# Latent attention: a unit's roots spread ahead of the weighing and scaled ahead of the next means, and a first preparation with each unit's chain in one step

## What is computed

```python
q = split_heads(rms_norm(c_q, mla_cq_norm) @ mla_w_uq, MLA_HEADS)
kv = split_heads(rms_norm(c_kv, mla_ckv_norm) @ mla_w_ukv, MLA_HEADS)
k_nope, v = jnp.split(kv, [MLA_NOPE_DIM], axis=-1)
k = jnp.concatenate([k_nope, k_rope_h], axis=-1)
q = rms_norm(q, mla_q_norm)
k = rms_norm(k, mla_k_norm)
q = jnp.concatenate([q[..., :MLA_NOPE_DIM], rope(q[..., MLA_NOPE_DIM:], cos, sin)], axis=-1)
k = jnp.concatenate([k[..., :MLA_NOPE_DIM], rope(k[..., MLA_NOPE_DIM:], cos, sin)], axis=-1)
o_mla = merge_heads(block_causal_attention(q, k, v)) @ w_branch_mla
g_fox, g_mla = jnp.split(jax.nn.sigmoid(gate_logit + b_gate), N_BRANCH, axis=-1)
```

## Time and profile before

| | us |
|---|---|
| median of 3 runs (2532.12 to 2543.33) | 2540.17 |
| the profiled execution | 2539.42 |
| its span, first to last instruction | 2537.6 |
| PE busy in the span | 2395.9 (94%) |
| DVE busy | 1423.5 (56%) |
| ACT busy | 958.0 (38%) |
| POOL busy | 508.5 (20%) |
| mean granted TensorE clock, as a share of full speed | 0.967 |

### The profile page before, as it was taken

How to read it: one execution, slowest core, us unless ns; L and a number is a source line. 1 busy time by engine, 2 the same in 40 slices (tenths; PEclk the granted TensorE clock), 3 DMA queues, 4 the chain that set the end, 5 groups by cost and what they waited for, 6 DMA issues and landing times. The chain is left out here.

```text
span 2537.6 us, 36864 instructions
## 1 busy us (share of the span) xinstructions
PE 2395.9 (94%) x14060; PEld 2124.4 (84%) x14060; DVE 1423.5 (56%) x2057; ACT 958.0 (38%) x1621; POOL 508.5 (20%) x632
## 2 busy tenths in 40 slices
PE   6899999999978999989899999989989999999999
PEld 6899999999968888878677777778877888887887
DVE  7655655655554574572455555544276666556553
ACT  5333333333334454442343333353343333334332
POOL 0032300000022442440233333332410332000000
PEclk8999999999988899989999999989999999999999
DMA  5356633375421000001111111023613656427553
GB/s 187 119 190 216 208 127 105 145 273 184 144 83 52 26 1 25 26 1 36 37 50 37 37 40 36 26 96 132 237 54 132 226 192 213 139 69 276 207 200 109
DMA packets 132698, 297.99 MB, mean 117 GB/s; under 512 B 10096, under 2 KB 57072, under 8 KB 129216
## 3 DMA queue, kind: packets, MB, share of 16 engines
q1 hardware_dynamic: 132544, 295.88, 33.6%
HBM read 206.99 MB, written 88.72 MB: 117 GB/s over the span
## 5 line engine op out<-in xcount | busy, mean ns | idle before, releaser
L1070 DVE TENSOR_TENSOR f_w_lo<-f_rw,f_w_hi 128x1024 fp32r<-128x1024 f32 x154 | 195.2, 1267 | 222.2 <-ACT f_w_hi L590 222.2
L833 PE MATMUL f_ps<-u_hi,f_w_hi 128*128 128x260 f32 (+1 forms) x1056 | 283.7, 323 | 25.9 <-DVE f_w_lo L1070 13.1
L833 PE MATMUL f_ps<-u_lo,f_w_hi 128*128 128x260 f32 (+1 forms) x1056 | 283.0, 323 | 0.0
L833 PE MATMUL f_ps<-u_hi,f_w_lo 128*128 128x260 f32 (+1 forms) x1056 | 282.7, 322 | 0.0
L590 ACT CAST f_w_hi<-f_rw 128x1024 fp32r<-128x1024 f32 x154 | 161.2, 1047 | 164.4 <-PE f_ps L833 157.2
L833 PE MATMUL f_ps<-f_far_hi,f_w_hi 128*128 128x260 f32 (+1 forms) x792 | 211.9, 322 | 8.7 <-DVE f_ev L1086 8.7
L833 PEld LDWEIGHTS f_ps<-u_hi,f_w_hi 128*128 128x128 f32 x1056 | 178.3, 192 | 42.2 <-DVE f_w_lo L1070 14.6
L833 PE MATMUL f_ps<-f_far_lo,f_w_hi 128*128 128x260 f32 (+1 forms) x792 | 210.9, 321 | 0.0
L833 PE MATMUL f_ps<-f_far_hi,f_w_lo 128*128 128x260 f32 (+1 forms) x792 | 210.7, 321 | 0.0
L833 PEld LDWEIGHTS f_ps<-u_lo,f_w_hi 128*128 128x128 f32 x1056 | 177.8, 192 | 14.3
L833 PEld LDWEIGHTS f_ps<-u_hi,f_w_lo 128*128 128x128 f32 x1056 | 177.7, 192 | 14.1
(11 more groups left out here) (392 smaller groups left out, 5954.0 us busy)
## 6 DMA issues: line engine op xcount, KB each, us to landing
f_rw<-in_gu SPq DMA_DIRECT2D x88, 512.0 KB, 4.4
f_rw<-kept_dsum SPq DMA_DIRECT2D x32, 704.0 KB, 4.7
f_rw<-kept_hid SPq DMA_DIRECT2D x33, 520.0 KB, 5.6
f_rw<-in_down SPq DMA_DIRECT2D x24, 704.0 KB, 4.3
f_rw<-kept_hid SPq DMA_DIRECT2D x33, 512.0 KB, 5.4
h_in<-in_wd SPq DMA_DIRECT2D x11, 1024.0 KB, 6.7
kept_dsum<-h_in SPq DMA_DIRECT2D x44, 256.0 KB, 3.0
h_out<-in_wd SPq DMA_DIRECT2D x11, 1024.0 KB, 7.2
```

Source lines behind the costliest of these rows:

```text
L833: last = nc.tensor.matmul(out[:, b, 0:N], w[:, c], u[:, b * N:(b + 1) * N], start=(j < 3 and k == 0 and i == 0), stop=(k == 3 and i == 2), ...
L1070: nc.vector.tensor_tensor(slot(w_lo, st), src, slot(w_hi, st).bitcast(F32), ALU.subtract).then_inc(wlo_done, 1)
```

## The change

In the heads, the spread of unit w-1 moves on PE from behind the sums of unit w to ahead of the weighing. On ACT the copy of the roots of unit w-1 moves ahead of the root of unit w. On DVE the means of unit w move from ahead of the rounding of the scores to behind the scaling of unit w-1, and the rotation (now `turn`) stands behind the means. In the first preparation each unit's projection, sums, spread and scaling all stand in one step, the rounding of unit w-1 stands ahead of the squares of unit w on ACT, and the tables of groups and of logit copies are new. Nothing is added or left out; only the order changes.

```diff
@@ tables of the first preparation
-        FIRST = {(w, x): 2 if 2 <= w < 6 else 1 - x if w >= 6 else 0 for w in range(14) for x in range(2)}
-        FIRST.update({(0, 0): 1, (0, 1): 5, (1, 0): 2})
+        FIRST = {(w, x): 0 for w in range(-1, 14) for x in range(2)}
+        FIRST.update({(-1, 0): 1, (-1, 1): 4, (0, 0): 1, (0, 1): 2, (5, 0): 1, (5, 1): 1})
+        FIRST.update({(w, x): 1 + 2 * x for w in range(1, 5) for x in range(2)})
+        FIRST.update({(w, 0): 1 for w in range(8, 14)})
...
-        COPY_FIRST = (2, 4, 6, 13)
+        COPY_FIRST = (0, 2, 4, 13)
@@ block.scalar
-            def early(p, h, w):
-                u = w - 3
+            def split_hi(p, h, u):
...
-            def late(p, h, w):
+            def root(p, h, w):
                 if w < NU:
                     upto(act, ms_done, NU, p, h, w + 1)
...
-                if 1 <= w <= NU:
-                    u = w - 1
+
+            def spread(p, h, u):
+                if 0 <= u < NU:
...
             def head(p, h, more=True, next_gate=True):
                 for w in range(NW):
                     if more:
-                        early(p, h + 1, w)
+                        split_hi(p, h + 1, w - 3)
                         copy_logits(p, h + 1, w)
                     exponential(p, h, w)
                     if more:
                         square(p, h + 1, w)
-                        late(p, h + 1, w)
+                        spread(p, h + 1, w - 1)
+                        root(p, h + 1, w)
+                        values_hi(p, h + 1, w)
                         gate_weights(p, h + 1, w, more=next_gate)
...
             for w in range(NW):
-                early(0, 0, w)
+                split_hi(0, 0, w - 1)
+                square(0, 0, w)
+                root(0, 0, w)
                 copy_logits(0, 0, w, COPY_FIRST)
-                square(0, 0, w)
-                late(0, 0, w)
+                spread(0, 0, w)
+                values_hi(0, 0, w)
@@ block.tensor
             def prepare(p, h, w):
-                if w < NU:
-                    sums(p, h, w)
-                if 1 <= w <= NU:
-                    broadcast(p, h, w - 1)
                 maxima(p, h, w, 2)
...
                     if more:
                         maxima(p, h + 1, w, 1)
                         gates(p, h + 1, w, 1)
+                    if more and 1 <= w <= NU:
+                        broadcast(p, h + 1, w - 1)
                     if shifted(p, h, w):
                         weigh(p, *shifted(p, h, w))
+                    if more and w < NU:
+                        sums(p, h + 1, w)
                     if more:
                         prepare(p, h + 1, w)
...
-            gates(0, 0, 0, 0, FIRST)
+            gates(0, 0, -1, 0, FIRST)
             latent_sum(pe, 8)
-            gates(0, 0, 0, 1, FIRST)
-            products(0, 0, 0)
-            prepare(0, 0, 0)
-            for w in range(1, NW):
+            gates(0, 0, -1, 1, FIRST)
+            for w in range(NU):
+                products(0, 0, w)
+                gates(0, 0, w, 0, FIRST)
+                sums(0, 0, w)
+                gates(0, 0, w, 1, FIRST)
+                broadcast(0, 0, w)
+            for w in range(NU, NW):
                 maxima(0, 0, w, 0)
-                if w < NU:
-                    products(0, 0, w)
                 gates(0, 0, w, 0, FIRST)
                 maxima(0, 0, w, 1)
-                gates(0, 0, w, 1, FIRST)
                 prepare(0, 0, w)
@@ block.vector (turn: the rotation's three instructions, cut out of scale)
             def early(p, h, w):
                 maxima(p, h, w, 0)
                 maxima(p, h, w, 1)
-                if w < NU:
-                    mean_squares(p, h, w)
-
-            def prepare(p, h, w):
+
+            def roots(p, h, w):
                 if 0 <= w - 3 < NU:
                     split_lo(p, h, w - 3)
                 if 1 <= w <= NU:
                     scale(p, h, w - 1)
+                if w < NU:
+                    mean_squares(p, h, w)
+                if 1 <= w <= NU:
+                    turn(p, h, w - 1)
+
+            def first_roots(w):
+                if w < NU:
+                    mean_squares(0, 0, w)
+                if 1 <= w <= NU:
+                    split_lo(0, 0, w - 1)
+                if w < NU:
+                    scale(0, 0, w)
+                    turn(0, 0, w)
+
+            def prepare(p, h, w):
                 maxima(p, h, w, 2)
...
                     nc.vector.tensor_copy(p_hi[:, w % 2, 0:n], p32[:, w % 2, 0:n]).then_inc(phi_done, 1)
                     if more:
+                        roots(p, h + 1, w)
                         prepare(p, h + 1, w)
...
             for w in range(NW):
                 early(0, 0, w)
+                first_roots(w)
                 prepare(0, 0, w)
```

More of the change, by code:

```diff
@@ L2365, in late, with values_hi @@
                     nc.scalar.copy(rs[:, 0:n], BC[:, 0:n]).then_inc(rs_done, 1)
+            def values_hi(p, h, w):
                 if w == V_STEP:
@@ L2637, in scale, with turn @@
                                                    rs[:, 0:n], ALU.mult, ALU.mult).then_inc(x_done, 1)
+                else:
+                    nc.vector.tensor_tensor(x[ROPE_ROWS], g.turn[0:ROPE, t0:t0 + n], rs[0:ROPE, 0:n], ALU.mult)
+                    nc.vector.scalar_tensor_tensor(x[0:NOPE], src[0:NOPE, 0:n], g.gains[0:NOPE, g.MK_COL:g.MK_COL + 1],
+                                                   rs[0:NOPE, 0:n], ALU.mult, ALU.mult).then_inc(x_done, 1)
+            def turn(p, h, u):
+                is_q, c = units[u]
+                t0, n = QK_TOKENS[c]
+                x = x32[:, u % 2, 0:n]
+                if is_q:
                     upto(dve, x_done, NU, p, h, u + 1)
@@ L2646, in scale @@
                                             ALU.add).then_inc(rope_steps, 1)
-                else:
-                    nc.vector.tensor_tensor(x[ROPE_ROWS], g.turn[0:ROPE, t0:t0 + n], rs[0:ROPE, 0:n], ALU.mult)
-                    nc.vector.scalar_tensor_tensor(x[0:NOPE], src[0:NOPE, 0:n], g.gains[0:NOPE, g.MK_COL:g.MK_COL + 1],
-                                                   rs[0:NOPE, 0:n], ALU.mult, ALU.mult).then_inc(x_done, 1)
             def split_lo(p, h, u):
```

## The result

| | kernel before | changed kernel |
|---|---|---|
| median | 2539.4 us (5 runs, 2532.1 to 2543.3) | 2559.8 us (5 runs, 2557.3 to 2566.4) |
| span of the profiled execution | 2537.6 us | 2557.7 us |
| mean granted clock | 0.967 | 0.962 |
| PE busy | 2395.9 us | 2411.8 us |

The ratio is 1.0089, with a 95% interval of 1.0072 to 1.0105: **slower, by about 20 us**. The forecast was 2533.3 with a range of 2523 to 2544, so the time lies outside it, and on the side to which 0.03 had been given.

A forecast was written before the change was run, and what follows sets the result against it. PE's matmuls were taken to bound the heads, leaving 17.0 us of waits to win. 2539.4 - 9.2 (heads) + 2.1 (newton) + 1.0 (first preparation) = 2533.3 us, chance 0.52, range 2523 to 2544.

The forecast's parts named there:

- What bounds the kernel: In the seven heads PE's matmuls bound; only gaps can be won, at most 17.0 us of waits.
- Products are free in time: In the heads, products are free 1.7 to 2.2 us after the spread, so their waits of 15.0 us go.
- The means come 0.35 us later: On DVE in the heads, means behind the scaling come 2.2 us after the spread instead of 1.85, nearly cancelling 0.46 won.
- The wait in step 3 gives back 8 us: Before the ninth group, gains of steps 2 and 3 are lost; logits-copy waits grow from 2.0 to some 8 us.
- The 54%: Share of one head's waits that stays won (1.59 of 2.93 us), carried to all seven heads as 9.2 us.
- Nothing in step 6: Late in each head: the 0.29 us before a group stays won; logits-copy waits were all expected in step 3.
- Newton, 2.1 us: POOL's newton step before unit 5's spread, slowed by DVE's rotation: 0.3 us lost per head, 2.1 us in all.
- rival C: Newton is held in the heads: each unit 5 spread waits 1.1 us, 7.7 in all; 2538.9 us, chance 0.13.
- The clock in the heads: PE in the seven heads was taken at full clock; the sum held no clock loss there.
- Rival D: New gaps in the first preparation pull TensorE's clock to half: 13.8 us lost, 2547.0 us, chance 0.10.
- The first preparation, 1.0 us: Before the heads: new waits of sums for ACT's squares, some 2.5 us in steps 1, 3 and 5; 1.0 us lost.
- Rival B: All waits in the heads go, 17.0 us won, and the first preparation is even: 2522.4 us, chance 0.25.

The follow-up runs named there:

- The best order: Changed heads with logits copies early, means ahead of scaling and the second copy behind the root, first preparation as before: 2520.7 us, 0.9919 against the kernel before.
- the kernel with the early copy: Changed kernel, first preparation as before, first two logits copies in the heads moved ahead of the root on ACT: 2522.3 us, 0.9943 against the kernel before.
- the squares first: Changed first preparation with ACT's squares ahead of the rounding: 2528.0 us with logits copies early in the changed heads, 2517.5 us with the best heads.
- the heads alone: The change made only in the heads, first preparation as in the kernel before: 2555.6 us, 1.0077 against the kernel before.
- the kernel before with the early copy: Kernel before, with only the first two logits copies in the heads moved ahead of the root on ACT: 2564.0 us, 1.0124.
- the finish in step 3: Changed kernel with the two instructions that finish the head before moved one step later on ACT and DVE: 2537.5 us, 1.0003 against the kernel before.

## Why the prediction was wrong, point by point

The profiled execution was to be 6.1 us shorter and is 20.1 longer. The 26.2 us between divide like this: 9.7 are waits in the heads (19.6 for the 7.8 + 2.1 of the sum), 15.3 the clock there, 5.2 the first preparation (6.2 for 1.0) and 0.6 the phases behind; the last head took 4.7 off.

**What bounds the kernel** was right: PE's matmuls, with 17.0 us to be won in the heads. The best order won 14.9 us of them.

**Products are free in time:** right, though by less than it seemed. 0.2 us of waits are left of 15.0. The interval from spread to free products was not 1.7 to 2.2 us but up to 2.7, since the scaling starts 1.63 us after the spread, not 1.03, and in the rows above the products come 2.89 us after it.

**The means come 0.35 us later (the term that failed first).** The sentence took the scaling to begin 0.50 us after the copy of roots. It left out that DVE rounds the scores in between, and that this rounding waits for the weighing, which the change itself puts behind the spread. The means came 2.72 us after the spread, where 2.2 were forecast, so the forecast that the two shifts in front of the group nearly cancel failed.

**The wait in step 3 gives back 8 us.** The mechanism, the place and the name were right, the size was not: 12.2 us in seven waits, 1.93 to 1.97 in the six heads with a finish, 0.52 in the first. The later means (0.5 us in six heads) and four waits of 0.22 us that stood in front of this group before, though not in the head that was read, make 4.0 of the 4.2 us. The 54% carried to all heads was that head's share; over all seven, 8.0 of the 17.0 us lie behind step 3, 47%.

**Nothing in step 6:** wrong. The copy for the seventeenth group hangs on the same chain of means, root and rounding, and its group waited 0.96 to 1.04 us in each head, 7.1 us. The working looked at step 6 for the newton step only.

**Newton, 2.1 us:** 0.2 us in the changed kernel, but only because the copy's wait stood beside it. Once that was gone, 7.8 us stood there, the size that rival C had been given (7.7). Part of that is luck: C had no late root, and an earlier root alone took all of the wait away, while leaving out the rotation took 2.0 us. The ground for taking 0.3 us was weak too. The newton instruction of the earlier trace rows shares only 0.06 us with the scaling. Two others there, at 1208.56 and 1208.84, do keep their 0.20 us beside it, but the scaling takes one input from PSUM (`mla_bank`) and the rotation both from SBUF, so they say little of the rotation. The rule of the Trainium skill, page SBUF — State Buffer, section Who interferes with whom (an instruction of DVE with two SBUF inputs contends with a GpSimd instruction that reads SBUF), agrees with the rows of POOL above: a newton instruction of 0.20 us took 0.57 and ended with the subtraction beside it. The one of 1.15 us in the earlier trace rows began 0.41 us before its subtraction, so there the rule accounts for the end and not for the whole length.

**The clock in the heads (the term that was missing).** The sum took the clock there as full without a reason, and this was the largest part: 15.3 us. Rival D named the mechanism, but put it in the first preparation alone, where it cost 6.8 us in place of its 13.8. The rows to suspect it were there: half clock in the kernel before stood in the first preparation, which has gaps of 1.4 and 1.9 us, and never in the heads, whose longest gap is 0.99. The working made one gap of 0.99 into a longer one and priced it at its own length. The size was not in those rows: of the five gaps of 1.4 to 1.9 us in that preparation one, of 1.37, was followed by a fall, against five of six of 1.9 us in the changed heads.

**The first preparation, 1.0 us:** the waits were as forecast (2.2, 2.4 and 1.8 us where three of 2.5 were expected), and in all PE waited as long as before there, 9.8 us. The clock behind them was not in the sum: 13.6 us more at half, 6.8 of the 7.25 us by which this stretch grew.

**Rival B** (all waits go) did not occur. That the kernel with the early copy took 2522.3 us, as B's 2522.4, is luck: its heads gave 7.8 us and not 17.0, and the rest came from outside them.

What stays open: why the last head with the start of the output gates holds 10.2 us at half clock in some profiles and up to 23.9 in others, which moves a time by some 7 us. It was 10.2 in all five with the change's first preparation, 10.2, 13.7, 17.1 or 23.9 in the seven with the old one, and 23.9 in the two with the squares first. Whether the first preparation has a part in this, no run was made to show. Open, too, is what besides its length makes a gap bring the clock down (last section).

## What to carry to other kernels

When a step is moved ahead on one engine, list what stands in front of its consumer on the next engine and what that waits for; here an unrelated rounding, tied to the work that had just been moved back, ate the lead. A gap on PE can cost more than its length: here most gaps of 1.9 us and more brought the clock down, and none under 0.95 us in the heads did. So many short waits were better than a few that sum them, and a wait that grows past every gap of its stretch needs a price for the clock as well, as a rival at least. And a small copy that frees a bank belongs where its engine is idle, ahead of work that waits for something later, but only if nothing more urgent queues behind it.

## What the runs showed of the hardware that was not expected

The granted clock fell to half (1.2 GHz) for 3.4 us or a multiple of it at most single gaps of 1.9 to 2.4 us in otherwise busy heads: at five of six in the changed kernel, five of six in the heads alone, and six of seven in the kernel before with the early copy, where PE waits for DVE and not for ACT. Most falls began behind the gap, four in its last 0.3 to 0.8 us. A wait of 1.93 us so cost 3.6 us in most heads.

Gaps of about 1 us are less clear. Of those of 0.96 to 1.06 us in front of a group in step 6, three of seven were followed by a fall in the changed kernel, four of seven in the heads alone and two of seven with the finish in step 3, in each case within 0.4 us of the gap's end. But of the 28 gaps of 0.97 to 1.14 us in front of the spread, in four kernels with the early copy, none was. In the heads of the kernel before none of its gaps was, of up to 0.99 us, and in no kernel a gap of the heads under 0.95 us. In the first preparation with the squares first, the same gaps of 1.5 and 1.6 us brought 17.1 us at half in one profile and none in the other. So a gap's length makes a fall more likely and does not decide it alone.
